# The spatial gate inside the first attention's side work, on two column halves, and the last two squares of a norm summed by TensorE

## The reference, cut to what matters

```
h = rms_norm(x, norm_mix_g);  z = h @ w_in
u, v, q, kv, gl = split(z)
# spatial gate, 8 groups of 64 features, 4 chunks of 128 tokens
v = layer_norm(gelu(v));  w = tril(sg_w)          # (8, 128, 128)
s[b,c,t,g,:] = sum_s w[g,t,s] * v[b,c,s,g,:] + sg_b[g,t]
a = gelu(u) * s
b = nsa_attention(q, kv, gl)                      # 8 heads, 3 branches
mixed = [rms_norm(a), rms_norm(b)];  x = x + mixed @ w_out
```

## Time and profile before

| | us |
| --- | --- |
| median of 3 runs (2761.8 to 2762.77) | 2761.8 |
| the profiled execution | 2760.01 |
| its span, first to last instruction | 2758.2 |
| TensorE busy | 2548.8 |
| VectorE busy | 1156.1 |
| ScalarE busy | 874.9 |
| GpSimd busy | 532.6 |

### The profile page before, as it was taken

One profiled execution on the slowest core, in us unless ns is written; L12 is line 12 of the kernel. 1 busy time (PEld: TensorE's weight loads), 2 busy tenths in 40 slices (PEclk: granted clock), 3 DMA queues, 4 the chain that ended last, 5 costly groups with the idle time before them and its releaser, 6 DMA issues.

```text
span 2758.2 us, 33891 instructions
## 1 busy us (share of the span) xinstructions
PE 2548.8 (92%) x13851; PEld 1979.4 (72%) x13851; DVE 1156.1 (42%) x1907; ACT 874.9 (32%) x1589; POOL 532.6 (19%) x398
## 2 busy tenths in 40 slices
PE   7888889899999898999989999999698999899998
PEld 5655667677788675578866888888465577678876
DVE  3645544553444426442266223223435533642433
ACT  3325542432222214432145211212324432532222
POOL 3004212321111212220022110122313210221023
PEclk8997999999999899999999999999789999999998
DMA  4231151344422210102200122122110123013232
GB/s 157 78 93 31 47 168 61 108 153 153 153 92 91 87 30 20 39 24 62 84 9 16 46 84 62 46 77 100 48 30 21 39 69 107 1 47 114 77 92 92
DMA packets 188636, 200.59 MB, mean 73 GB/s; under 512 B 15640, under 2 KB 183288, under 8 KB 187970
## 3 DMA queue, kind: packets, MB, share of 16 engines
q1 hardware_dynamic: 184866, 178.23, 21.0%
q10 hardware_dynamic: 3616, 20.19, 1.9%
HBM read 187.92 MB, written 10.49 MB: 72 GB/s over the span
## 4 chain that ended last, share of the span: by engine, by line
PE 82%; DVE 7%; ACT 5%; POOL 3%; issue 3%; DMA 1%; ACTq 0%; POOLq 0%; SPq 0%; DVEq 0%
PE PS L682 20%; PE PS L683 20%; PE PS L685 20%; PE PS L764 5%; PE PS L791 4%; PE PS L777 2%; PE PS L1110 2%; DVE ST L1778 1%; ACT SA L1266 1%; PE PS L726 1%; DVE WL L1710 1%; POOL RB L2412 1%; PE PS L833 1%; PE PS L889 1%; PE PS L860 1%
## 5 line engine op out<-in xcount | busy, mean ns | idle before, releaser
L682 PE MATMUL PS<-HH,WH 128*128 128x512 f32 x2144 | 797.0, 372 | 36.7 <-POOL HL L2417 19.6
L683 PE MATMUL PS<-HL,WH 128*128 128x512 f32 x2144 | 764.6, 369 | 0.0
L685 PE MATMUL PS<-HH,WL 128*128 128x512 f32 x2144 | 692.4, 367 | 0.0
L1710 DVE TENSOR_TENSOR WL<-WB,WH 128x2048 fp32r<-128x2048 f32 (+2 forms) x150 | 313.2, 2088 | 640.6 <-ACT WH L1199 632.7
L682 PEld LDWEIGHTS PS<-HH,WH 128*128 128x128 f32 x2144 | 405.4, 189 | 155.4 <-issue 29.7
L683 PEld LDWEIGHTS PS<-HL,WH 128*128 128x128 f32 x2144 | 405.9, 189 | 73.9 <-issue 1.9
L685 PEld LDWEIGHTS PS<-HH,WL 128*128 128x128 f32 x2144 | 366.7, 189 | 46.6
L1199 ACT ACTIVATE WH<-WB 128x2048 fp32r<-128x2048 f32 (+2 forms) x150 | 256.3, 1708 | 362.3 <-PE PS L685 290.5
L2437 POOL TENSOR_SCALAR SA<-SA,ST 128x768 f32<-128x768 f32 (+3 forms) x80 | 141.1, 1764 | 451.8 <-DVE ST L1792 451.8
L2412 POOL TENSOR_TENSOR RB<-RB,SA 128x512 f32<-128x512 f32 (+2 forms) x68 | 92.7, 1363 | 429.6 <-ACT SA L1216 428.0
L1266 ACT ACTIVATE SA<-PS,ST 128x768 f32<-128x768 f32 (+3 forms) x160 | 118.8, 743 | 94.7 <-DVE ST L1778 94.3
(11 more groups left out here) (324 smaller groups left out, 3420.5 us busy)
## 6 DMA issues: line engine op xcount, KB each, us to landing
WB<-in_w_in_dram SPq DMA_DIRECT2D x67, 1024.0 KB, 5.3
WB<-in_w_ff_dram SPq DMA_DIRECT2D x32, 1024.0 KB, 5.5
WB<-in_w_mod_dram SPq DMA_DIRECT2D x24, 1024.0 KB, 5.3
WB<-in_w_branch_dram SPq DMA_DIRECT2D x24, 512.0 KB, 3.5
WB<-in_w_o_dram SPq DMA_DIRECT2D x8, 1024.0 KB, 5.6
XTc<-xd ACTq DMA_DIRECT2D x2, 3072.0 KB, 10.1
WB<-in_cmp_w_dram SPq DMA_DIRECT2D x4, 1024.0 KB, 5.5
WB<-in_w_mkv_dram SPq DMA_DIRECT2D x4, 1024.0 KB, 5.2
```

The lines of the kernel that those rows point to most:

```text
L682: pe.matmul(D[0:m, d + o:d + o + w], h, xh[:, o:o + w], start=first, stop=False)
L683: pe.matmul(D[0:m, d + o:d + o + w], h, xl[:, o:o + w], start=False, stop=False)
L685: t = pe.matmul(D[0:m, d + o:d + o + w], lo, xh[:, o:o + w], start=False, stop=last)
L1710: dve.tensor_tensor(WL[s % NH][:, 0:b.kt, 0:b.cols], WB[b.n % NW][:, 0:b.kt, 0:b.cols], WH[s % NH][:, 0:b.kt, 0:b.cols].bitcast(F32), ALU. ...
```

## The change

Three things are altered. First, the squares of the slices 6 and 7 of `x` are no longer added by GpSimd: TensorE sums the accumulator (now of slices 0 to 5) and both squares by twelve products in place of four, all into the same four columns. Second, the gate's products are cut by group: one product of 64 value features by 128 columns for each group and chunk, the two groups of a pair on the two halves of the output partitions. So VectorE adds the bias to all 128 partitions in one operation. Third, the gate becomes the first four pieces of the attention's side work, on slot 4 like the rest. ScalarE and GpSimd get four empty pieces, and ScalarE waits for the last gate product before the squares of `am`. The matrices `wT` and the bias `SGB` get a place in memory of their own, apart from the attention's buffers. The pieces of the diff follow one another as memory, TensorE, ScalarE, VectorE, GpSimd.

```diff
-                    SGB, wT = sb("SGB", 128, 4, 128, scope=s1b), sb("wT", 128, 8, 128, scope=s1b)
...
+                with ExitStack() as s1c:
+                    SGB, wT = sb("SGB", 128, 4, 128, scope=s1c), sb("wT", 128, 8, 128, scope=s1c)
...
-            sum_columns("x", 8, NX, ("rbc", "x"))
+            D = slot(("norm", "x"), ("rbc", "x"))
+            pe.wait_ge(*at("nadd", "x", 5))
+            parts = [RB[rb["x"]]]
+            for f in (6, 7):
+                parts.append(SA[sa["x", f]])
+            pe.wait_ge(*at("sq", "x", 7))
+            for i, part in enumerate(parts):
+                for c in range(4):
+                    t = pe.matmul(D[:, c:c + 1], part[:, c * 128:(c + 1) * 128], cm("ones")[:, 0:1], start=i + c == 0, stop=i == 2,
+                                  skip_group_check=True)
+            t.then_inc(*done("nsum", "x"))
...
-            pe.wait_ge(*at("vln", 3))
-            pe.wait_ge(*at("wt", 1))
-            for i in range(4):
-                D = slot(("sg", i), ("sgs", i))
-                for c in range(4):
-                    t = pe.matmul(D[:, c * 256:(c + 1) * 256], vt[:, c, i * 128:(i + 1) * 128], wT[:, 2 * i:2 * i + 2, :], start=True, stop=True)
-                t.then_inc(*done("tr", "sg", i))
+            def gate():
+
+                pe.wait_ge(*at("vln", 3))
+                pe.wait_ge(*at("wt", 1))
+                for i in range(4):
+                    D = slot(("sg", i), ("sgs", i))
+                    for c in range(4):
+                        for h in range(2):
+                            t = pe.matmul(D[64 * h:64 * h + 64, c * 128:(c + 1) * 128], vt[:, c, i * 128 + 64 * h:i * 128 + 64 * h + 64],
+                                          wT[:, 2 * i + h, :], start=True, stop=True)
+                    t.then_inc(*done("tr", "sg", i))
+                    yield
...
             def aside():
+                yield from gate()
                 yield from paced_norm("am", 4, 512)
...
-                sq("x", f, XTa[:, f, :], ("xTc", f), ("ud", 3))
+                sq("x", f, XTa[:, f, :], ("xTc", f), ("ud", 3) if f < 6 else ("nsum", "x"), by_pe=f > 5)
...
             def aside():
+                for _ in range(4):
+                    yield
+                act.wait_ge(*at("tr", "sg", 3))
...
+            def gate():
+                dve.wait_ge(*at("sgb"))
+                for i in range(4):
+                    D = taken(("sg", i), ("am", i))
+                    dve.wait_ge(*at("tr", "sg", i))
+                    dve.tensor_tensor(D[:, 0:512].rearrange("p (a b) -> p a b", b=128), P("sg", i)[:, 0:512].rearrange("p (a b) -> p a b", b=128),
+                                      SGB[:, i, :].unsqueeze(1).to_broadcast([128, 4, 128]), ALU.add).then_inc(*done("sgs", i))
+                    dve.wait_ge(*at("sgs", i))
+                    dve.wait_ge(*at("ug", i))
+                    dve.tensor_tensor(uT[:, i, :], uT[:, i, :], D[:, 0:512], ALU.mult).then_inc(*done("am", i))
+                    yield
...
-            for f in range(1, 8):
+            for f in range(1, 6):
                 add_sq("x", f, NX)
...
             def aside():
+                for _ in range(4):
+                    yield
                 yield from paced_norm("am", 4, 512, lambda f: HL[:, f, 0:NX], lambda f: HH[:, f, 0:NX])
```

More of the change, by code:

```diff
@@ L1204, in begin, with sq @@
                     split_hi(s)
-            def sq(N, f, src, ready, freed=None, k1=128):
+            def sq(N, f, src, ready, freed=None, k1=128, by_pe=False):
                 n = src.shape[-1]
@@ L1212, in sq @@
                     D = taken(rb, RB, N, freed)
+                elif by_pe:
+                    D = taken(sa, SA, (N, f), freed)
                 else:
@@ L2041, in vector_program @@
             together(gate_u(), compress())
-            for i in range(4):
-                D = taken(("sg", i), ("am", i))
-                dve.wait_ge(*at("tr", "sg", i))
-                dve.wait_ge(*at("sgb"))
-                for h in range(2):
-                    lo, hi = h * 64, h * 64 + 64
-                    t = dve.tensor_tensor(D[lo:hi, 0:512].rearrange("p (a b) -> p a b", b=128),
-                                          P("sg", i)[lo:hi, :].rearrange("p (a b) -> p a b", b=256)[:, :, h * 128:(h + 1) * 128],
-                                          SGB[lo:hi, i, :].unsqueeze(1).to_broadcast([64, 4, 128]), ALU.add)
-                t.then_inc(*done("sgs", i))
-                dve.wait_ge(*at("sgs", i))
-                dve.wait_ge(*at("ug", i))
-                dve.tensor_tensor(uT[:, i, :], uT[:, i, :], D[:, 0:512], ALU.mult).then_inc(*done("am", i))
             cin = VC[:, rows["c"] // 128, rows["c"] % 128:rows["c"] % 128 + 16].rearrange("p (a b) -> p a b", b=8)
```

## The result

The changed kernel is slower by a little: median 2771.86 us of 8 runs (2766.46 to 2776.02), against 2763.39 of 8 runs of the kernel before on the same chip (2761.80 to 2765.97). The ratio is 1.0028 with an interval of 1.0017 to 1.0039. I had predicted 2759.1 and a range up to 2765.0, so the time lies outside it, on the side to which I gave 0.08.

A forecast was written before the change was run, and what follows sets the result against it. TensorE, busy for 92% of the span, was taken as the bound. The terms -1.3 - 2.6 - 1.5 + 2.7 gave -2.7 us, so 2759.1 us on the median, with a range of 2752.0 to 2765.0.

The forecast's parts named there:

- Gate, end: End of the attention: 1.5 us gained up to the last scores, then 2.7 us lost before and at `wo`.
- -1.5 us where TensorE is the bound: Up to the last scores: TensorE has done one modulation product and one turn less, so they come 1.5 us earlier.
- the chain at its end: From last scores to `wo`: the fourth modulation product, load and weight split stand behind the scores, costing +1.3 us.
- First norm: Kernel start: two fewer GpSimd additions, TensorE sums in 24 passes; -1.3 us, ends -1.4 and +1.1.
- Gate, head: Attention start: scores begin 9.0 us earlier, most given back to gate batches; -2.6 us, ends -4.8 and 0.
- The 1.5 as the price at half clock: Gate batches: 16 passes were taken to cost 1.5 us at half clock, from 32 in 2.99.
- GpSimd's stall: Early attention: additions for the norm `am` hold up a turn of scores by 3.26 us; claimed neither gained nor lost.
- the chain to `wo` and its clock: Last scores to `wo`: longer chain +1.3 us and half-clock restart 1.4, together +2.7, ends -2 and +5.
- B: Rival: inside the attention nothing moves, only the start gains; 2760.5 us, or 2762.9 if the clock falls; chance 0.14.
- C: Rival: clock falls to 0.50 in the column sum, gate's two steps and `wo` restart; 2769.2 us; chance 0.09.
- The condition under which I called the prediction failed: Last tile of `u` to `wo` changing by other than -4 to +1 us, or a later stage by over 1.

The follow-up runs named there:

- `e_shift4`: Kernel before with four empty pieces ahead of the attention's side work on every engine, gate left in place; 2775.42 us, ratio 1.0052.
- `x_mv_early`: Changed kernel with the weight split of the first block of the memory's values four pieces earlier, at its old step; 2770.08 us, ratio 1.0030.
- `e_start`: Kernel before with only the first norm changed, twelve products in place of four, gate as before; 2762.11 us, ratio 0.9998.
- `e_form`: Kernel before with the gate's products cut by column halves and one bias addition, gate still ahead of the attention; 2758.96 us, ratio 0.9984.
- `r_after_pair`: Changed kernel with the memory norm's eight squares done two to a piece, giving 100 pieces again; 2759.89 us, ratio 1.0000.
- `e_gate`: Changed kernel with the first norm summed as before, so only the gate's part is changed; 2771.09 us, ratio 1.0031.
- `e_startform`: Kernel before with the changed first norm and the gate's form by column halves, gate left ahead of the attention; 2758.77 us, ratio 0.9989.
- `p_shift6`: Kernel before with six empty pieces ahead of the attention's side work, three steps late; 2770.98 us, ratio 1.0034.
- `p_shift2`: Kernel before with two empty pieces ahead of the attention's side work, one step late; 2770.97 us, ratio 1.0025.
- `p_after6`: Changed kernel with two more empty pieces behind the gate and one fewer behind each of the last four modulation products; 2766.07 us, ratio 1.0010.

## Why the prediction was wrong

**The step that failed** is "Gate, end", with its term "-1.5 us where TensorE is the bound". I took the two steps' delay of the side work as free within the attention, and as a small gain at its end. `e_shift4` measures that delay alone: from `u` to `wo` it costs 201.22 - 193.25 = 8.0 us (and 0.52% in the total). My terms for the same were -1.5 and, for the chain at its end, +1.3, together -0.2. In the changed kernel itself, the stretch from the third step's maxima to the end of the last scores, in which the -1.5 should have shown, took 171.4 us (210.15 to 381.54) against 165.3 (211.53 to 376.80): +6.1. I looked at what stood beside the first steps and the last, and had ordered rows of both. I did not look at the steps between, where each weight split met another kind of step than before, although the order of instructions and the trace had a sign of it: a split of 2.29 us on VectorE, ahead of a scaling that TensorE waits for. The size could not have been read from the one split, as `x_mv_early` shows.

**First norm, -1.3.** The local term was right and even small. 24 passes took 2.76 us where I had 3.0, the stretch was at full clock, and the stage of `kc` began 2.2 us earlier (39.78; 41.96 before). From the about 60 cycles that the Trainium skill (TensorEngine Tiling (Array Packing), Performance Considerations, Instruction Overhead) gives for a matmul, an added pass would be 25 ns at 2.4 GHz, an estimate; the row has 115. (The prediction made a gain of some 2.5 us of that estimate; with 1.05 us for the eight passes of the earlier trace rows it is 3.0.) What failed is that all that follows hangs on it: in the changed kernel's profile the half clock came at another place (85.7) and took 2.8 us there; `e_start` shows no gain in the total.

**Gate, head, -2.6.** Right: 3.2 us at the third step's maxima, batches of 1.09 us (I had 1.02 to 1.5), and four additions of 0.69. The 1.5 as the price at half clock was misread: the 2.99 us of the earlier trace rows lie in a stretch with a mean clock of 0.63, not 0.50. It did not matter, since the batches ran at full clock. Wrong was that GpSimd's stall is neither gained nor lost: 3.26 us became 0.64. In `e_shift4` that wait is 0.64 us as well, so the 8.0 us of the delay are what is left after this gain.

**Gate, end, +2.7 for the chain to `wo` and its clock.** The mechanism was right, its size short. The distance grew by 2.2 us and not 1.3: the fourth modulation product ended 3.4 us behind the last scores (3.9 in the prediction), the load landed 5.9 behind it (5.4), and the low half of the activations took 1.75 us, not 0.75, beside an addition of 1.65 on GpSimd. The `wo` stage paid 3.4 us for the clock, where I had 1.4.

**The rivals.** B said that the later steps wait on GpSimd and weight splits at fixed distances from the side work, and had the right place, but no loss: it took the distances as fixed, and the waits behind the splits differ with the kind of step. C had the sign and nearly the size (2769.2), by the wrong way: the clock was 1.00 in the column sum and in the gate's two steps (201.2 to 209.0). It was right on the restart of `wo`, which is 3.4 of the 8.5 us. The condition under which I called the prediction failed, a length from `u` to `wo` that changes by over +1 us, is met with +5.1.

What makes the +5.1: the gate's form gives 3.9 at the head (`e_form`), and 6.0 from `u` to `wo` in its profile; the delay costs 8.0; the rest, +3.1, would be the cost of the gate in the side work against ahead of it. `r_after_pair` against `e_form` has 3.8 us for the same (191.03 against 187.25). But these are single profiles, and by that of `e_gate` (196.0) the rest is 0.8. In the totals `r_after_pair` (1.0000) and `e_startform` (0.9989), whose gate stands ahead, have intervals that overlap. So a cost of the gate's place by itself is not shown.

**Open.** How much of the 11 us in steps 23 to 38 is the wait and how much the clock was not separated. The idle time there grew by 5.6 us, and the rest goes with the half clock, since its instructions are nearly the same. That the clock fell because of the waits is argued from their sequence in the rows, and no kernel held one and changed the other. With the same wait of 2.8 us behind the third split, the changed kernel has 10.2 us at half clock and `e_gate` 3.4 (338.7 to 342.1).

## What to carry to other kernels

Where side work is laid into a loop whose steps differ, what is put at the head of the list moves all behind it, and its price can lie in the phase of the long operations against the kinds of steps; test it with empty pieces, which cost nothing to write, before the real work is moved. Win the pieces back elsewhere in the list: that took the loss away here. A move by a whole period shortened the stretch with the splits, but `p_shift6` was still 0.34% slower. And try a better form of a piece in its old place first: here that gave 0.16% (`e_form`), and with the move the kernel lost 0.31% (`e_gate`).

## What the runs showed of the hardware

A pass with one column, 128x1 with its load of 128 columns of weights, took 0.115 us at full clock (24 in 2.76). A batch of 16 passes of 64x128 on alternating halves took 1.09 us (0.068 each), and the 32 passes of 128x256 that it replaces had 7.07 in all.

Where the granted clock falls is not fixed in a program. With the same code ahead of it, `u` ended at 198.46 (before), 197.05 (`e_shift4`), 196.74 (`p_shift6`) and 196.78 (`p_shift2`). With the changed first norm it was at 200.30 (after), 198.09 (`x_mv_early`), 198.00 (`p_after6`) and 196.03 (`r_after_pair`). So a profile places one execution to within about 2 us either way there, and a gain of 1 or 2 us can't be read from two of them. All behind the `wo` stage took 2310.5 (before) to 2318.3 us (`p_shift2`) with the same code. Half clock came to 128 us in the first and 141 in the second.

TensorE waited 2.81 us at 336.8 to 339.6; the clock was at 0.50 from 338.3 on and stayed there for the 8.9 us of work that followed. In `r_after_pair` a wait of 1.68 us (to 326.67) was followed by 3.4 us at 0.50, and in `x_mv_early` one of 1.60 (to 328.32) by 6.8. In the kernel before, the wait of 1.15 us behind the third split was followed by no fall, and in `p_shift6` the wait of 1.59 behind the second was not either (1.00 from 310.4 to 340.9). I had not expected a wait under 3 us inside dense work to cost as much again behind it; that it is the wait which does it is not shown.
